# End of the second mixer in token-block order, with the gate factors folded on GpSimd

## What is computed

```python
# x: 256 tokens x 1024; two token blocks of 128
attn_out = mla_attention(...)                      # 8 heads x 64 = 512 features
hm = mlstm(mq, mk, mv, ig, fg)                     # 4 heads x 128 = 512 features
hm = (hm - mean(hm)) * rsqrt(var(hm) + EPS)        # per token and head
hm = hm.reshape(B, S, 512) * mh_norm_g
ml_out = (hm + ml_skip * xc) * silu(z)
x = x + concatenate([attn_out, ml_out]) @ w_o      # w_o: 1024 x 1024
x = x + hier_moe(rmsnorm(x), ...)                  # 32 experts, 2 per token
x = x + (p @ w_ple) * sigmoid(rmsnorm(x) @ w_ple_gate)
return rmsnorm(x)
```

## Time and profile before

| what | us |
|---|---|
| median of 3 runs | 714.3 (713.69 to 718.03) |
| profiled execution, whole | 716.88 |
| its span, first to last instruction | 715.2 |
| TensorE busy in the span | 654.9 (92%) |
| VectorE busy | 351.6 (49%) |
| ScalarE busy | 272.1 (38%) |
| GpSimd busy | 48.5 (7%) |
| mean granted TensorE clock | 0.977 of full speed |

### The profile page before, as it was taken

One profiled execution on the slowest core, in us unless ns is written; L12 is line 12 of the kernel. 1 busy time (PEld: TensorE's weight loads), 2 busy tenths in 40 slices (PEclk: granted clock), 3 DMA queues, 4 the chain that ended last, 5 costly groups with the idle time before them and its releaser, 6 DMA issues.

```text
span 715.2 us, 10872 instructions
## 1 busy us (share of the span) xinstructions
PE 654.9 (92%) x4314; PEld 482.8 (68%) x4317; DVE 351.6 (49%) x622; ACT 272.1 (38%) x431; POOL 48.5 (7%) x72
## 2 busy tenths in 40 slices
PE   4999999799999999998999969899999986688895
PEld 3999987699999999984987858554444441224342
DVE  5686964777777777667594454521111110002223
ACT  5764453566555544556828311200111110010243
POOL 1000000400000000002447000000000000000000
PEclk9999999999999999999999989999999999989998
DMA  9844542757555555109333097979599999999901
GB/s 325 301 157 154 200 149 65 246 179 244 182 176 176 176 176 176 59 1 365 121 118 118 1 379 311 367 310 431 225 430 429 424 432 426 428 425 427 392 15 59
DMA packets 54344, 174.75 MB, mean 244 GB/s; under 512 B 4646, under 2 KB 29346, under 8 KB 47906
## 3 DMA queue, kind: packets, MB, share of 16 engines
q1 hardware_dynamic: 53632, 172.54, 63.1%
q10 hardware_dynamic: 674, 1.69, 0.6%
HBM read 173.17 MB, written 1.05 MB: 244 GB/s over the span
## 4 chain that ended last, share of the span: by engine, by line
PE 75%; DMA 13%; DVE 7%; ACT 3%; issue 1%; DVEq 0%; ACTq 0%
PE ps L1640 14%; PE ps L1641 14%; PE ps L1642 14%; DMA arena<-in_w_moe_dram 13%; PE ps L2134 6%; PE ps L2216 4%; PE ps L2144 4%; PE ps L2120 3%; PE ps L2169 3%; PE ps L1829 2%; PE ps L1887 1%; PE ps L1977 1%; DMA hh<-in_conv_ffn_dram 1%; PE ps L1928 1%; DVE hh L1003 1%
## 5 line engine op out<-in xcount | busy, mean ns | idle before, releaser
L1640 PE MATMUL ps<-hT_high,w_up_high 128*128 128x256 f32 x352 | 99.7, 283 | 1.8 <-DVE w_up_low L1185 1.8
L1642 PE MATMUL ps<-hT_high,w_up_low 128*128 128x256 f32 x352 | 99.6, 283 | 0.0
L1641 PE MATMUL ps<-hT_low,w_up_high 128*128 128x256 f32 x352 | 99.6, 283 | 0.0
L1640 PEld LDWEIGHTS ps<-hT_high,w_up_high 128*128 128x128 f32 x352 | 67.5, 192 | 2.7 <-DVE w_up_low L1185 2.3
L1641 PEld LDWEIGHTS ps<-hT_low,w_up_high 128*128 128x128 f32 x352 | 67.5, 192 | 0.4
L1642 PEld LDWEIGHTS ps<-hT_high,w_up_low 128*128 128x128 f32 x352 | 67.5, 192 | 0.0
L1185 DVE TENSOR_TENSOR w_up_low<-W,w_up_high 128x1024 fp32r<-128x1024 f32 x44 | 52.8, 1229 | 24.0 <-ACT w_up_high L774 24.0
L774 ACT CAST w_up_high<-W 128x1024 fp32r<-128x1024 f32 x44 | 44.6, 1046 | 28.7 <-PE ps L1642 28.7
L932 ACT ACTIVATE arena<-ps 128x256 f32<-128x256 f32 x9 | 3.4, 383 | 121.6 <-PE ps L2134 121.6
L1640 PE MATMUL ps<-h_high,dense_high 128*128 128x256 f32 x160 | 45.7, 286 | 0.0
L1641 PE MATMUL ps<-h_low,dense_high 128*128 128x256 f32 x160 | 45.3, 283 | 0.0
(11 more groups left out here) (449 smaller groups left out, 1303.9 us busy)
## 6 DMA issues: line engine op xcount, KB each, us to landing
W<-in_w_moe_dram SPq DMA_DIRECT2D x25, 2048.0 KB, 19.6
arena<-in_w_moe_dram SPq DMA_DIRECT2D x19, 2048.0 KB, 25.2
W<-in_w_up_dram SPq DMA_DIRECT2D x22, 1024.0 KB, 8.1
W<-in_w_in_dram SPq DMA_DIRECT2D x8, 2048.0 KB, 11.0
W<-in_w_down_dram SPq DMA_DIRECT2D x11, 1024.0 KB, 5.0
hh<-in_w_moe_dram SPq DMA_DIRECT2D x4, 2048.0 KB, 28.4
W<-in_w_out_dram SPq DMA_DIRECT2D x2, 2048.0 KB, 8.3
W<-in_w_o_dram SPq DMA_DIRECT2D x2, 2048.0 KB, 7.9
```

Of the source, the lines that this page charges most:

```text
L1640: pe.matmul(o, lhs[0], rhs[0], start=first, stop=False, skip_group_check=True)
L1641: pe.matmul(o, lhs[0], rhs[1], start=False, stop=False, skip_group_check=True)
L1642: return pe.matmul(o, lhs[1], rhs[0], start=False, stop=last_k, skip_group_check=True)
```

## The change

TensorE, VectorE and ScalarE work is put in another order, and one VectorE multiply of each block goes to GpSimd, for both blocks at once:

- TensorE: `attend(2)` stands ahead of `num(3)`; the rows of block 0 are turned ahead of `attend(3)`; block 0's first output half then starts on `y1_low` 4 alone; block 1's rows are turned between the two halves of block 0, and `turn_hm` stands between the two halves of block 1.
- VectorE: the bn_stats and bn_aggr pairs leave `divide` and become `moments(h)`, called for heads 0 and 1 after `attended(1)`, for heads 2 and 3 at the end. `attended(2)` stands between `divide(2)` and `divide(3)`; `lower_out` of block 0 between `divide(3)` and `attended(3)`; `lower_out` of block 1 between the normalisations of the two blocks.
- ScalarE: the square root of the variances stands between the copies of the two blocks.
- The gates: (hm g + s) z is computed as hm (g z) + (s z). GpSimd makes s z in xcT's place, then g z in szT's, once the skip is ready; VectorE then needs two operations for each block where it needed three.

```diff
@@ gpsimd, after the low parts of w_o
+            pool.wait_ge(sig("skip_ready"), at("skip_ready", 4))
+            pool.tensor_tensor(xcT[:], xcT[:], szT[:], ALU.mult).then_inc(sig("gates_folded"), 1)
+            pool.wait_ge(sig("gates_folded"), 1)
+            pool.tensor_tensor(szT[:], szT[:], par_c("mh_norm_g_2", 0, 4).unsqueeze(2).broadcast_to([P, 4, SEQ]),
+                               ALU.mult).then_inc(sig("gates_folded"), 1)
@@ scalar
             for b in range(TB):
                 act.wait_ge(sig("oT_done"), at("oT_done", b + 1))
                 act.copy(h1[0][:, 0:4, b * P:(b + 1) * P], v3(ps[:, b, :], 4)).then_inc(sig("y1_high"), 1)
-            act.wait_ge(sig("mvar_ready"), 1)
-            act.activation(mstd, mstd, ACT.Sqrt, bias=epsc[:]).then_inc(sig("mstd_ready"), 1)
+                if b == 0:
+                    act.wait_ge(sig("mvar_ready"), 1)
+                    act.activation(mstd, mstd, ACT.Sqrt, bias=epsc[:]).then_inc(sig("mstd_ready"), 1)
@@ vector, divide(h): its end becomes a function of its own
+            def moments(h):
+
                 dve.wait_ge(sig("hm_ready"), h + 1)
                 for b in range(TB):
                     link(dve.bn_stats(bns[:, 2 * h + b, :], hmt[:, b, h * P:(h + 1) * P]))
...
@@ vector, the order
             attended(0)
             attended(1)
+            moments(0)
+            moments(1)
             weigh(3)
             divide(2)
+            attended(2)
             divide(3)
-            attended(2)
+            lower_out(0, 0, 0, v3(ps[:, 0, :], 4))
             attended(3)
+            moments(2)
+            moments(3)
             link(dve.tensor_copy(mstd, mmv[:, :, 1]))
...
                     dve.tensor_scalar(v, v, mmv[:, 2 * h + b, 0:1], mstd[:, 2 * h + b:2 * h + b + 1],
                                       ALU.subtract, ALU.mult).then_inc(sig("hmn_ready"), 1)
-            for b in range(TB):
-                lower_out(b, 0, b, v3(ps[:, b, :], 4))
-            dve.wait_ge(sig("skip_ready"), at("skip_ready", 4))
+                if b == 0:
+                    lower_out(1, 0, 1, v3(ps[:, 1, :], 4))
+            dve.wait_ge(sig("gates_folded"), 2)
             for b in range(TB):
                 dve.wait_ge(sig("hmT_done"), at("hmT_done", b + 1))
                 y = hT[:, 4:8, b * P:(b + 1) * P]
-                link(dve.tensor_tensor(y, v3(ps[:, 2 + b, :], 4),
-                                       par_c("mh_norm_g_2", 0, 4).unsqueeze(2).broadcast_to([P, 4, P]), ALU.mult))
+                link(dve.tensor_tensor(y, v3(ps[:, 2 + b, :], 4), szT[:, :, b * P:(b + 1) * P], ALU.mult))
                 if b == 1:
                     lower_out(2, 4, 0, hT[:, 4:8, 0:P])
-                link(dve.tensor_tensor(y, y, xcT[:, :, b * P:(b + 1) * P], ALU.add))
-                dve.tensor_tensor(y, y, szT[:, :, b * P:(b + 1) * P], ALU.mult).then_inc(sig("ym_ready"), 1)
+                dve.tensor_tensor(y, y, xcT[:, :, b * P:(b + 1) * P], ALU.add).then_inc(sig("ym_ready"), 1)
@@ tensor
             num(2)
+            attend(2)
             num(3)
-            attend(2)
-            attend(3)
-            for b in range(TB):
+
+            def turn_o(b):
+
                 pe.wait_ge(sig("o_ready"), 3 + b)
                 for k in range(4):
                     last = pe.transpose(ps[:, b, k * P:(k + 1) * P], otok[:, b, k * P:(k + 1) * P], ident[:])
                 last.then_inc(sig("oT_done"), 1)
+
+            turn_o(0)
+            attend(3)
...
-            for b in range(TB):
-                pe.wait_ge(sig("y1_low"), 3 + b + 1)
-                for half in range(2):
-                    last = out_product(b, half, range(4))
-                if b == 0:
-                    turn_hm()
-            last.then_inc(sig("half_used"), 1)
+            pe.wait_ge(sig("y1_low"), 3 + 1)
+            out_product(0, 0, range(4))
+            turn_o(1)
+            out_product(0, 1, range(4))
+            pe.wait_ge(sig("y1_low"), 3 + 2)
+            out_product(1, 0, range(4))
+            turn_hm()
+            out_product(1, 1, range(4)).then_inc(sig("half_used"), 1)
```

More of the change, by code:

```diff
@@ L1419, in _, with lower_out @@
                               ALU.subtract).then_inc(sig("nm_ready"), 1)
+            def lower_out(n, k, b, src):
+                o = (slice(None), slice(k, k + 4), slice(b * P, b * P + P))
+                dve.wait_ge(sig("y1_high"), 3 + n + 1)
+                dve.tensor_tensor(h1[1][o], src, h1[0][o].bitcast(F32), ALU.subtract).then_inc(sig("y1_low"), 1)
             weigh(0)
```

## The result

The changed kernel takes 709.89 us (median of 8 runs, 707.05 to 711.41). Over the same series the kernel before has a median of 717.75 us (8 runs, 713.69 to 718.91), and the ratio is 0.9904 with a 95% interval of 0.9883 to 0.9924. By that ratio the change saves 6.9 us, within 1% by a hair. The two medians are 7.9 us apart; the means of the executions, 716.6 and 709.8 us, with which the ratio goes, are 6.8 apart. The forecast, 706.8 against 714.3, is a ratio of 0.9895, inside that interval; but in microseconds the measured median lies 0.4 us above the upper end of the range, 709.5, and faster by over 1% had been given more chance than the case that came. The profiled execution took 710.28 us, its span is 708.6 (before 715.2), the mean clock 0.979.

The account below looks back on a forecast made before the run. TensorE was taken to bound everything before the weight stream's last run. An earlier start of 6.3 us plus 1.74 for the clock less 0.45 for transposes gave 7.5 us: 714.3 to 706.8 us, range 704.8 to 709.5.

Parts of the forecast that it names:

- What bounds the kernel: TensorE bounds everything before the weight stream's last unbroken run, which starts after the stillness at 504 to 508 us.
- The start of the first half: Block 0's first products on TensorE start at 416.0 instead of 422.29, 6.3 us earlier, once its low part is ready.
- The inner waits: TensorE's waits inside the changed region are all met; two thin margins could cost 0 to 0.6 us, taken as 0.
- (a): TensorE's wait for block 1's low part, y1_low 5: seen at 421.6, wanted at 422.0, met by 0.4 us.
- (c): TensorE's wait for y1_low 6 ahead of the second half: 428.5 against 428.7, met by 0.2 us.
- The fold: GpSimd's two gate multiplies take 2.4 us each; divide(0) on VectorE loses 1.3 us, the program nothing.
- The clock term: Block 0's first 24 matmuls run at the second 24's pace: gain 1.74 us, other bound 0.
- one for one: Whatever TensorE gains ahead of the expert rounds moves the weight stream earlier by the same amount.
- rival 2: Order holds but is worth less: clock falls around 416 to 419 or waits are missed; 5.8 to 7.0 us, chance 0.22.
- Rivals 3 and 4: 3: weight stream hides the gain, 0 to 2 us, chance 0.09; 4: clock stays 0.50, 716.0 or 725.0 us, chance 0.04.

Follow-up runs that it names:

- latelow: Changed kernel with the moments of heads 2 and 3 put ahead of block 0's low part again on VectorE: 712.81 us, ratio 0.995.
- fold: Kernel before, in its old order, with the gates folded on GpSimd and two VectorE operations for each block: 717.41 us, ratio 1.0007.
- fill: Kernel before with 16 extra bf16 matmuls, results thrown away, in TensorE's 3.98 us wait for the first low part: 716.92 us, ratio 1.0001.
- both: Kernel before with 16 filler matmuls in the 3.98 us wait and 10 more ahead of the first expert round: 714.44 us, ratio 0.9963.
- after3: Changed kernel, unchanged, timed once more in the last series: 708.18 us, ratio 0.9858.
- warm2: Changed kernel with 10 more filler matmuls ahead of the first expert round, timed again in the last series: 708.95 us, ratio 0.9867.
- before2: Kernel before, unchanged, run once more: 717.26 us, ratio 1.0001.
- before3: Kernel before, unchanged, run once more in the last series: profile span 714.2 us, expert rounds 211.58 us.
- warmold: Kernel before with 10 more filler matmuls ahead of the first expert round: 715.05 us, ratio 0.9987.
- nofold: Changed kernel with the gates not folded: GpSimd's two multiplies out, VectorE's three operations for each block back: 710.25 us, ratio 0.9891.

## Why the prediction was right and where it failed

- **What bounds the kernel**: right. The stillness of the weight stream moved from 504 to 498 us and the last big product with it (679.25 to 672.64). Between these two profiles the gain went through one for one, because both had a slow round.
- **The start of the first half**: predicted 416.0; 417.44 with nm 1.55 us late is 415.89. It is set by block 0's low part (latelow: 2.2 us later for 2.2 us of work put ahead).
- **The inner waits**: (a) low part of block 1 ready at 422.25 + 0.68 = 422.93, wanted at 423.46, met by about 0.4 us, with 0.15 for the hand-over, as said; (c) 429.06 + 0.69 = 429.75 against 430.18, met by 0.3 us likewise with the fold and missed by 0.35 without it (predicted 0.5).
- **The fold**: GpSimd 2.36 and 1.89 us, bounds 1 to 2.8. The held VectorE operation ended at 401.75 + 0.98 = 402.73, with GpSimd's second instruction (402.71). By the rule of the Trainium skill, SBUF — State Buffer, section "Who interferes with whom", it had to; the trace agrees. It lost 0.8 us by it (0.98 against 0.16), where 1.3 had been forecast. Cost to the program nothing (fold, 1.0007).
- **The clock term and "one for one"**: in place the clock term was 1.74 us or more (fill 2.0 on average), so it was not too large. The step of the mechanism that failed is "what TensorE gains ahead of the expert rounds moves the stream too, one for one": fill gained 2.0 us locally and its ratio is 1.0001. The 2.9 us wait ahead of the first expert round was there in both kernels, and the clock behind it was low in every profile of the new order without extra fillers, but in 1 of 4 of the old. The trace of before, the only one at hand, happened to be that one, so its 5.44 us looked like a constant. The ground that the prediction gave for its clock term, "the drop followed only the long gap", also leaves out other low stretches of that trace, among them 367.9 to 371.4 us, with TensorE busy, and 466.9 to 470.3 us, behind the wait of 3.03 us. Against the usual execution of before, the change gains 7.9 us up to p (41.2 against 33.3) and by the stages gives back about 1.6 us in the rounds (213.2 against 211.6), which leaves 6.3 us, up to 1 us more if the early first product belongs to the new order. The ratio's 6.9 us, with 5.4 to 8.4 as its interval, has room for that and does not tell it from 7.9 or from the forecast 7.5: that the whole change gives something back is argued from the stages and from fill and both, not shown by its own times.
- **The base** is what put the time outside the range, and it is the term of the sum that was mis-sized. The forecast subtracted from 714.3, the median of three runs, while the profiled execution that gave every row had taken 716.88. The eight runs of before have 717.75, 3.4 us more, and in the four later series 717.07, 716.08, 716.82 and 717.78. From 716.88 the sum gives 716.88 - 7.5 = 709.4, 0.5 us below the measured 709.89. The range of 704.8 to 709.5 gave 1 us for the median where three runs had spread over 4.3. So the forecast 706.8 missed by 3.1 us: 3.4 of base, less the 0.4 by which the medians' 7.9 exceeds 7.5. That the whole gain came out so near to 7.5 is in part luck: by the stages, a clock term and an early start that were larger than foreseen and the loss in the rounds work against each other.
- **The chances**: by the ratio rival 2, worth less, is what came, with 6.9 us in its band of 5.8 to 7.0 (the medians' 7.9 is nearer to the forecast), but not by the causes that it names: no clock fell at 416 us and no wait was missed. Its time, 707.3 to 708.5, did not come, since it had the same base. Rivals 3 and 4 did not come: the gain was not hidden, and no window between 417 and 425 us was below 1.00.

The run warm, the changed kernel with ten fillers more, has 0.9874 and 0.9867 of before in two series. The changed kernel alone has 0.9904, 0.9904 and 0.9858 in three, and in the one series that has both, after3 is even a little ahead of warm2. That warm is the faster of the two is suggested by the stages (1.1 to 1.7 us in the rounds) and not shown by the times.

## What to carry to other kernels

A rebuilt timeline of the region, from durations and hand-overs of the trace, gave the local gain to 0.2 us; what went wrong lay outside it. Subtract from the time of the execution that the durations come from, and let the range be as wide as the runs shown are spread. And when a gain comes from the clock, look for the next wait downstream and ask at which clock the work behind it will now start: it may hand the gain back. Ten fillers there were never followed by the low clock, and cost nothing that could be measured.

## What the runs showed of the hardware

- In the stage ahead of nm TensorE's granted clock was 0.50 from 367.9 to 371.4 us in before, from 367.5 to 374.4 us in after and not at all in before2, although TensorE was busy without a break there (in after from 365.9 us on): windows of 2 us from 368 to 374 us had a clock of 0.50 in after, and 1.00 in before2. The same 32 matmuls took 7.17, 8.64 or 10.07 us, the stage up to nm 376.4 to 380.3 us.
- The 16 matmuls ahead of the first dense product took 3.65 or 5.59 us (before, before2), the first product coming at 17 or at 19.4 us; the record of the clock begins at 12.95 and at 17.82 us, and a window that lies ahead of it prints 1.00 without a record.
- A wait of 2.0 us (latelow, one profile) left the clock alone. With one of 2.9 to 3.0 us ahead of the first expert round a low stretch began, in the wait or up to 1.3 us behind it, in 9 of 12 profiles. In one of 4.0 us (before, before2, before3, fold, warmold) it always did.
- VectorE's operation of 128x2 with its inputs in SBUF took 0.98 us beside GpSimd's multiply and 0.16 us without it (after, nofold), and ended 0.02 us behind GpSimd's instruction.
